# Query turns moved into the projection banks, between the gate tiles

## The reference

```
h = rmsnorm(x, norm1_g)
q, k, v, cb, cc, cx, g_attn, g_conv = split(h @ w_in)
q, k = partial_rope(rmsnorm(q)), partial_rope(rmsnorm(k))
attn = windowed_gqa(q, k, v, sink)      # 8 heads, 2 KV heads, band of 3 blocks of 128
conv = cb * conv3(cc * cx)
merged = sigmoid(g_attn) * (attn @ w_attn_proj) + sigmoid(g_conv) * (conv @ w_conv_proj)
x = x + merged @ w_out
x = x + hierarchical_moe(rmsnorm(x))
```

## Time and profile before

| quantity | value |
|---|---|
| median of 3 runs | 2042.31 us (2041.8 to 2044.8) |
| profiled execution, its own time | 2044.8 us |
| its span | 2043.0 us |
| TensorE busy with matmuls | 1889.1 us, 92% |
| VectorE, ScalarE, GpSimd busy | 49%, 40%, 28% |
| granted TensorE clock, mean | 0.973 of full speed |

### The profile page before, as it was taken

How to read it: one execution, slowest core, us unless ns; L and a number is a source line. 1 busy time by engine, 2 the same in 40 slices (tenths; PEclk the granted TensorE clock), 3 DMA queues, 4 the chain that set the end, 5 groups by cost and what they waited for, 6 DMA issues and landing times.

```text
span 2043.0 us, 27997 instructions
## 1 busy us (share of the span) xinstructions
PE 1889.1 (92%) x10942; PEld 1470.2 (72%) x10942; DVE 1004.2 (49%) x1998; ACT 815.1 (40%) x1506; POOL 567.7 (28%) x403
## 2 busy tenths in 40 slices
PE   7999999998785999988999999999789999999997
PEld 6878879832221793457888888888767797888886
DVE  2160443521111525963366677822466714776777
ACT  5123551211111423264455444342266725454442
POOL 2244332011111220144422113243045543113211
PEclk9999999998988999999999999999899999999999
DMA  6223103699998330201123223321500012223321
GB/s 231 83 84 123 42 1 145 274 388 419 420 420 317 104 106 18 83 1 43 42 83 124 83 83 124 130 60 42 124 2 1 2 42 78 88 83 124 124 83 42
DMA packets 82324, 248.48 MB, mean 122 GB/s; under 512 B 12259, under 2 KB 15523, under 8 KB 69904
## 3 DMA queue, kind: packets, MB, share of 16 engines
q1 hardware_dynamic: 75936, 231.54, 30.6%
q0 software_dynamic: 4880, 9.89, 1.4%
q10 hardware_dynamic: 1376, 5.25, 0.6%
HBM read 241.89 MB, written 12.58 MB: 125 GB/s over the span
## 4 chain that ended last, share of the span: by engine, by line
PE 48%; DVE 4%; issue 2%; ACT 2%; POOL 0%; DVEq 0%; ACTq 0%
PE psA L1427 33%; PE psT L1585 2%; PE psS L1585 2%; PE psO L1585 2%; PE psO L1967 2%; PE psT L2004 1%; DVE x L2556 1%; PE psS L1995 1%; PE psA L1536 1%; PE psO L1487 1%; PE psT L1519 1%; PE psA L1995 1%; DVE scr L3390 1%; ACT big L2037 1%; PE psA L1911 1%
## 5 line engine op out<-in xcount | busy, mean ns | idle before, releaser
L1136 POOL TENSOR_TENSOR w_slot<-ring,w_slot 128x1024 fp32r<-128x1024 f32 (+2 forms) x80 | 208.5, 2619 | 542.3 <-ACT w_slot L2037 542.0
L1427 PE MATMUL psA<-hT_hi,w_slot 128*128 128x512 f32 x992 | 307.9, 389 | 0.0
L2037 ACT ACTIVATE w_slot<-ring 128x1024 fp32r<-128x1024 f32 (+2 forms) x178 | 192.0, 1088 | 176.9 <-PE psA L1427 77.0
L1427 PEld LDWEIGHTS psA<-hT_hi,w_slot 128*128 128x128 f32 x992 | 186.3, 188 | 38.7
L1427 PE MATMUL psA<-hT_lo,w_slot 128*128 128x512 f32 x496 | 192.9, 389 | 0.0
L2556 DVE TENSOR_TENSOR x<-psA,x 128x512 f32<-128x512 f32 (+1 forms) x204 | 121.0, 622 | 146.3 <-PE psA L1427 142.5
L2556 DVE TENSOR_TENSOR w_slot<-ring,w_slot 128x1024 fp32r<-128x1024 f32 x98 | 119.8, 1224 | 116.1 <-ACT w_slot L2037 116.1
L2037 ACT ACTIVATE big<-psA 128x512 f32<-128x512 f32 (+6 forms) x149 | 66.2, 469 | 272.0 <-PE psA L1427 140.2
L1427 PE MATMUL psA<-w_slot,hid_part 128*128 128x512 f32 x672 | 161.4, 389 | 0.0
L2037 ACT ACTIVATE scr<-scr,stat 128x384 f32<-128x384 f32 (+3 forms) x224 | 124.4, 556 | 71.2 <-DVE stat L3390 39.4
L1427 PEld LDWEIGHTS psA<-w_slot,hid_part 128*128 128x128 f32 x672 | 126.2, 188 | 26.1
(11 more groups left out here) (378 smaller groups left out, 4427.5 us busy)
## 6 DMA issues: line engine op xcount, KB each, us to landing
ring<-in_mlp_w SPq DMA_DIRECT2D x32, 2048.0 KB, 8.2
ring<-in_w_in SPq DMA_DIRECT2D x8, 2048.0 KB, 8.0
ring<-in_w_gate_e SPq DMA_DIRECT2D x14, 1024.0 KB, 17.1
ring<-in_w_up_e SPq DMA_DIRECT2D x14, 1024.0 KB, 21.6
ring<-in_w_down_e SPq DMA_DIRECT2D x13, 1024.0 KB, 27.2
big<-in_w_down_e SPq DMA_DIRECT2D x12, 1024.0 KB, 27.5
ring<-in_ab_w_in SPq DMA_DIRECT2D x5, 2048.0 KB, 8.0
scr<-in_w_down_e SPq DMA_DIRECT2D x7, 1024.0 KB, 24.9
```

What stands on the lines that cost most here:

```text
L1136: nc.gpsimd.tensor_tensor(part(w_lo, c), raw_piece(c), part(w_hi, c).bitcast(F32), ALU.subtract)\
L1427: ins = pe.matmul(o, a, b, start=(at == 1), stop=(at == 3 * len(terms)))
L2037: return nc.scalar.activation(o, i, f, **kw)
```

## The change

The six turns become jobs in psA0 and psA1, and stand between the gate tiles: q turns 0 and 1, gate tile 0, q turns 2 and 3, gate tile 1, both k turns, gate tile 2. ScalarE reads them out in the same order. VectorE's last operation on each turn now raises `proj_evacuated`, in place of `query_lo`; TensorE waits before the attention until both k turns are read out. In all, ten jobs stand where four stood, so later jobs keep their banks.

The last gate tile gets the sigmoid function at step 2 of the attention, as the other tiles; VectorE's addition and reciprocal go away. The small operation that loads the exponential's table early goes away. The four casts `conv_hi` on VectorE move from steps 3 to 6, one each, to steps 2 and 3, two each.

```diff
-               ("gc0", 4), ("gc1", 4), ("mergec", KD), ...
+               ("gc0", 4), ("turn_qa", 2), ("gc1a", 1), ("turn_qb", 2), ("gc1b", 1), ("turn_qc", 2), ("gc1c", 2), ("mergec", KD), ...
+def second_gate(m):
+    return JOBS["gc1" + "abcc"[m]] + m // 3
+def query_turn(j):
+    return JOBS["turn_q" + "abc"[j // 2]] + j % 2
...
 # TensorE
             pe.wait_ge(heads_ready, 1)
             for j in range(4):
-                for t in range(NT):
-                    ins = pe.transpose(query_bank(j)[:, t * P:(t + 1) * P], qk[:, t, j * P:(j + 1) * P], ident)
-                ins.then_inc(query_turned, 1)
+                turn(query_turn(j), [qk[:, t, j * P:(j + 1) * P] for t in range(NT)])
+                if j % 2:
+                    gate_tile(j // 2)
             for g in range(2):
-                for t in range(NT):
-                    for half in range(2):
-                        ins = pe.matmul(query_bank(4 + g)[HD * half:HD * (half + 1), t * P:(t + 1) * P],
-                                        qk[:, t, 512 + HD * g:512 + HD * (g + 1)], ident, start=True, stop=True)
-                ins.then_inc(query_turned, 1)
-            for m in range(3):
-                gate_tile(m)
-            pe.wait_ge(query_lo, 6)
+                turn_twice(query_turn(4 + g), [qk[:, t, 512 + HD * g:512 + HD * (g + 1)] for t in range(NT)])
+            gate_tile(2)
+            copied_all(pe, "turn_qc", 2)
...
 # ScalarE
             for j in range(4):
-                act.wait_ge(query_turned, j + 1)
-                A(band_q[0:HD, j, :], query_bank(j)[0:HD, :], ACT.Copy)
-                A(band_q[HD:P, 4 + j, :], query_bank(j)[HD:P, :], ACT.Copy).then_inc(stack_hi, 1)
-            act.wait_ge(query_turned, 6)
+                n = query_turn(j)
+                product(act, n)
+                A(band_q[0:HD, j, :], bank(n)[0:HD, :], ACT.Copy)
+                A(band_q[HD:P, 4 + j, :], bank(n)[HD:P, :], ACT.Copy).then_inc(stack_hi, 1)
+                if j % 2:
+                    conv_gate(1, j // 2)
+            product(act, query_turn(5))
             for g in range(2):
-                A(band_k[:, g, 0, :], query_bank(4 + g)[:, :], ACT.Copy).then_inc(stack_hi, 1)
-            for m in range(3):
-                conv_gate(1, m)
-            A(small[:, 310:311], ident[:, 0:1], ACT.Exp)
+                A(band_k[:, g, 0, :], bank(query_turn(4 + g))[:, :], ACT.Copy).then_inc(stack_hi, 1)
+            conv_gate(1, 2)
...
                 if step == 2:
-                    evac(JOBS["gc1"] + 3, gc[:, KD - 1, :], f=ACT.Exp, scale=-1.0)
+                    conv_gate(1, 3)
...
 # VectorE, for each turn: the last lo operation
-                    .then_inc(query_lo, 1)
+                    .then_inc(proj_evacuated[n % 2], 1)
...
-                if 3 <= step < 7:
-                    if step == 3:
-                        product(dve, JOBS["gc1"] + 3)
-                    copied(dve, JOBS["cb"] + step - 3)
-                    nc.vector.tensor_copy(conv_hi[:, step - 3, :], conv[:, step - 3, :]).then_inc(conv_in_hi, 1)
-                if step == 9:
-                    copied(dve, JOBS["gc1"] + 3)
-                    link(ts(gc[:, KD - 1, :], gc[:, KD - 1, :], 1.0, op0=ALU.add))
-                    link(nc.vector.reciprocal(gc[:, KD - 1, :], gc[:, KD - 1, :]))
+                if step in (2, 3):
+                    if step == 2:
+                        product(dve, second_gate(3))
+                    for m in range(2 * step - 4, 2 * step - 2):
+                        copied(dve, JOBS["cb"] + m)
+                        nc.vector.tensor_copy(conv_hi[:, m, :], conv[:, m, :]).then_inc(conv_in_hi, 1)
```

More of the change, by code:

```diff
@@ L138 @@
                ("norm0", KD), ("kv", NT), ("q", 2 * NT), ("cc", 4), ("cx", 4), ("cb", 4), ("ga", KD),
-               ("gc0", 4), ("gc1", 4), ("mergec", KD), ("turn_o0", 4), ("mergea", KD), ("wo", 3 * NT), ("tail1", NT + KD),
+               ("gc0", 4), ("turn_qa", 2), ("gc1a", 1), ("turn_qb", 2), ("gc1b", 1), ("turn_qc", 2), ("gc1c", 2), ("mergec", KD), ("turn_o0", 4), ("mergea", KD), ("wo", 3 * NT), ("tail1", NT + KD),
                ("ranks", 1), ("table", 1), ("moe", 5 * PAIRS),
@@ L154 @@
 SPLIT_NORMS = (3, 4, 5)
+def second_gate(m):
+    return JOBS["gc1" + "abcc"[m]] + m // 3
+def query_turn(j):
+    return JOBS["turn_q" + "abc"[j // 2]] + j % 2
 def job(stage, i):
+    if stage == "gc1":
+        return second_gate(i)
     if stage == "nq":
@@ L485, in build @@
         stack_hi = sem("stack_hi")
-        query_turned = sem("query_turned")
-        query_lo = sem("query_lo")
         p_scores = sem("p_scores")
@@ L661, in ax_bank @@
             return (psT + psO)[t]
-        def query_bank(j):
-            return (psT + psO + psS)[j]
         def index_bank(c):
@@ L1607, in gate_tile @@
                 wh, wl = piece(SPLIT_AT["gc1"] + m)
-                split_product(JOBS["gc1"] + m, T, [(wh[:, k, :], wl[:, k, :], hT_hi[:, k, :], hT_lo_early[:, k, :])
+                split_product(second_gate(m), T, [(wh[:, k, :], wl[:, k, :], hT_hi[:, k, :], hT_lo_early[:, k, :])
                                                   for k in range(KD)])
@@ L1630, in conv_gates @@
                 if step == CONV_STEP:
-                    copied_all(pe, "gc1", 4)
+                    copied_all(pe, "gc1c", 2)
                     pe.wait_ge(conv_in_hi, 4)
@@ L2232, in conv_gate @@
             def conv_gate(c, m):
-                evac(JOBS[f"gc{c}"] + m, gc[:, 4 * c + m, :], f=ACT.Sigmoid)
+                evac(job(f"gc{c}", m), gc[:, 4 * c + m, :], f=ACT.Sigmoid)
                 then_split(SPLIT_AT[f"gc{c}"] + m)
@@ L2891, in _ @@
             for j in range(4):
+                n = query_turn(j)
                 dve.wait_ge(stack_hi, j + 1)
-                tt(band_q[HD:P, j, :], query_bank(j)[0:HD, :], band_q[0:HD, j, :].bitcast(F32), ALU.subtract)
-                tt(band_q[0:HD, 4 + j, :], query_bank(j)[HD:P, :], band_q[HD:P, 4 + j, :].bitcast(F32), ALU.subtract)\
-                    .then_inc(query_lo, 1)
+                tt(band_q[HD:P, j, :], bank(n)[0:HD, :], band_q[0:HD, j, :].bitcast(F32), ALU.subtract)
+                tt(band_q[0:HD, 4 + j, :], bank(n)[HD:P, :], band_q[HD:P, 4 + j, :].bitcast(F32), ALU.subtract)\
+                    .then_inc(proj_evacuated[n % 2], 1)
             for g in range(2):
+                n = query_turn(4 + g)
                 dve.wait_ge(stack_hi, 5 + g)
-                tt(band_k[:, g, 1, :], query_bank(4 + g)[:, :], band_k[:, g, 0, :].bitcast(F32), ALU.subtract).then_inc(query_lo, 1)
+                tt(band_k[:, g, 1, :], bank(n)[:, :], band_k[:, g, 0, :].bitcast(F32), ALU.subtract)\
+                    .then_inc(proj_evacuated[n % 2], 1)
             def conv_part(step):
-                if 3 <= step < 7:
-                    if step == 3:
-                        product(dve, JOBS["gc1"] + 3)
-                    copied(dve, JOBS["cb"] + step - 3)
-                    nc.vector.tensor_copy(conv_hi[:, step - 3, :], conv[:, step - 3, :]).then_inc(conv_in_hi, 1)
-                if step == 9:
-                    copied(dve, JOBS["gc1"] + 3)
-                    link(ts(gc[:, KD - 1, :], gc[:, KD - 1, :], 1.0, op0=ALU.add))
-                    link(nc.vector.reciprocal(gc[:, KD - 1, :], gc[:, KD - 1, :]))
+                if step in (2, 3):
[4 more added lines that the diff above has]
+                        nc.vector.tensor_copy(conv_hi[:, m, :], conv[:, m, :]).then_inc(conv_in_hi, 1)
                 m = (step - CONV_STEP) // 3 - 1
```

## The result

| | before | after |
|---|---|---|
| device time, median of 4 runs each (us) | 2042.05 (2039.28 to 2044.8) | 2057.86 (2056.71 to 2058.74) |
| ratio, 95% interval | | 1.0083 [1.0067, 1.0098] |
| profiled execution (us) | 2044.8 | 2061.94 |
| its span, its mean granted TensorE clock | 2043.0, 0.973 | 2060.1, 0.968 |

The changed kernel is slower, by 17.0 us by the ratio (13.7 to 20.0). The forecast was +11.4 (2053.7 us) with a range up to 2056.8. The direction and the three waits came as forecast; the size did not, and the median lies 1.06 us outside the range. Each profiled execution is the slowest of its kernel in this comparison; they lie 17.1 us apart.

A forecast was written before the change was run, and what follows sets the result against it. TensorE was taken to set the pace, with no gap. Stalls 8.4, clock 2.3, table load 1.3 and reciprocal -0.6 sum to +11.4 us, on the median 2042.3 giving 2053.7 us; range for 8 in 10 is 2050.3 to 2056.8.

The forecast's parts named there:

- The three stalls: Before gate tiles 0, 1 and 2, TensorE waits for shared banks to be read; +8.4 us in sum, 7.4 to 9.4 allowed.
- The third table load: In the attention's head, the load after the sigmoid stands on ScalarE's path and shifts the attention; +1.3 us.
- The reciprocal's 0.6 us: In the attention, removing VectorE's reciprocal on the last gate tile gives back 0.59 us; -0.6 us in the sum.
- signs of being wrong: Gate tile 1 starting before 208 us, or the shift at the first score not found again at the end.
- The clock: TensorE's clock falls behind both query-turn stalls, 1.15 us each, +2.3 us; nothing for the k turns.
- The clock does not fall behind the stalls: Rival for the query-turn stalls: no clock fall, or only in their idle part; +9.1 us, 2051.4 us; chance 0.22.
- The stalls are worse: Rival: both clock falls in full, casts and a slower table switch on the path; +14.5 us, 2056.8 us; chance 0.12.
- a slower switch of tables: In the attention's head, a drain of about 1.38 us on every switch would make the table-load term 2.7 us.
- the casts: At step 2, VectorE's two casts put item 3's mask about 0.9 us later; hidden, otherwise up to 0.9 us.
- Absorbed: Rival: a load behind the attention that comes at its own time absorbs the delay; 2042 to 2045 us; chance 0.03.
- faster: Rival: all of ScalarE's 3.02 us wait for the reciprocal comes back and stalls do not exist; 2040.6 us; chance 0.02.
- both falls behind the stalls to be sure: At the query-turn stalls, if transposes do not count as clock work, both falls are sure; sum up by at most 0.8 us.

The follow-up runs named there:

- experiment 4: The changed kernel with twelve unused matmuls of 512 columns before gate tiles 0 and 1 each; 2055.64 us, +12.1 us against the kernel before.
- experiment 12: The changed kernel with unused filler matmuls in the query-turn waits, attention head, behind the attention and around the MLPs; 2049.95 us, +6.9 us against the kernel before.
- experiment 2: The kernel before with only the last gate changed: sigmoid, two casts per step, no add, reciprocal or early table load; 2046.22 us, +3.1 us.
- experiment 7: The kernel before without the addition and reciprocal of the last gate tile, so part of the gate is wrong; 2044.40 us, +1.2 us (-0.6 to 2.9).
- experiment 1: The changed kernel with the old last gate, casts and early table load, so only the turns moved; 2057.17 us, +13.5 us against the kernel before.
- experiment 5: The kernel before with the sigmoid gate and its table loads, no reciprocal, casts one per step; 2047.54 us, +3.9 us.
- experiment 9: The kernel before with one 128x1 Sigmoid ahead of ScalarE's evacuation at step 2, two more table loads in its wait; 2043.71 us, +0.8 us (-1.0 to 2.7).
- experiment 10: The kernel before with one 128x1 Sigmoid right behind ScalarE's evacuation at step 2, two more table loads on its path; 2046.42 us, +4.3 us.
- experiment 3: The kernel before with gate tiles between the turns as in the changed kernel, but turns in their own banks; 2041.91 us, -0.6 us (-2.4 to 1.2).
- experiment 8: The kernel before with unused 160-column matmuls around the turns behind the attention and before both MLPs' first products; 2037.06 us, -5.5 us.
- experiment 11: The kernel with only the turns moved, ScalarE reading each turned tile before the weight piece; 2052.85 us, +10.0 us against the kernel before.

## Why the prediction was wrong

**Right.** The three stalls, place by place: 2.89, 2.88 and 1.51 us of waiting where about 2.9, 2.8 and 1.4 were forecast, and together they put the first score back by 8.8 us, without the clock, instead of 8.4. That sum was built from the rows of this place in their new order, with the hand-over lag of 0.05 us from another layer where such turns share a bank, and experiments 4 and 12 confirm it. The third table load was priced at 1.3 us and took 1.4: item 5, still ahead of the low stretch, comes 10.84 us behind the first score instead of 9.45. The reciprocal's 0.6 us stand in the traces of experiments 2 and 7 to the tenth, though no median can show them. One of the prediction's own signs of being wrong did come: the shift at the first score, 10.9 us, is not the one at the end, 17.1. Most of the difference arises in the head and behind the attention; at 300 us the shift is 16.5. Nothing behind absorbed the delay: the queue's wait for the merge product, 92.5 us in the earlier trace rows, is no shorter now, 98.1:

```profile
SPq L1125 <- PE psA L1433: 98.1, 1, 98.1
```

**The step that failed** is the term "The clock", priced at 2.3 us; the trace pair has about 7.3 us for it: 2.5 at the turns, 3.1 in the attention's head and 1.7 behind the attention. It looked for falls only behind the two stalls of the query turns. There it was nearly right in size: 2.5 us in the changed kernel (one fall of 6.8 us, and none behind the first stall), about 3 in experiment 1 (two falls). That size is partly luck in the changed kernel: one fall of twice the length came in place of two. What it left out are the falls at places where the change adds no stall of microseconds:

- The head of the attention. The prediction counted the third table load by its 1.28 us alone. TensorE's work there is short matmuls with waits of 0.5 to 0.9 us between; the load makes them a little sparser, and the clock falls for 6.8 us. The trace of the changed kernel has 3.1 us for it, beside 1.4 for the load (4.5 at item 10). Experiments 2 and 5 show the same without the moved turns, and 9 and 10 show that a longer path on ScalarE does it.
- The turns behind the attention. The earlier trace rows were read as the price of a fall, but not as a place where the fall can get longer: 3.4 us low before, 10.2 us now, 1.7 us more by the 49th matmul. Experiment 1 has 6.8 us there and 1.1 us more. Why it gets longer is open: the change adds no wait there, and traces of kernels with neither the moved turns nor the sigmoid differ there too (3.4 us before, 6.8 in experiments 3 and 9, none in 7).

**How much of the 17 us is clock.** Twice the missing share of the granted clock times the span is the time spent at 1.2 GHz: 108 us for the kernel before (mean over 29 runs), 119 for the turns alone, 126 for the changed kernel (mean of seven executions at 0.968 to 0.972), 87 for experiment 8 and 92 for experiment 12. At most half of such a time is lost, where TensorE sets the pace. The changed kernel has 18 us more of it, worth up to 9 us. Waits, load and reciprocal are 8.8 + 1.4 - 0.6 = 9.6, and 17.0 - 9.6 leaves 7.4. That is within the bound, and near the 7.3 of the traces, but the clock's share was shown by removal only in part: the fillers of experiment 4 brought 2.5 us in the trace and took 17.0 to 12.1 in the ratios; all of them (experiment 12) took 17.0 to 6.9, which is 4.6 us more than the 5.5 that such fillers bring in the kernel before.

**The rivals.** "The clock does not fall behind the stalls" is out, by experiment 1. "The stalls are worse", at 2056.8, came nearest in size and mostly for a wrong reason: its 3.1 us for two full falls are what experiment 1 shows, but the rest of its extra came from a slower switch of tables and from the casts. In the changed kernel the load at 234.84 takes 1.28 us and the next activation starts at 236.13, so there is no drain of 1.38 us such as the Trainium skill gives in "ScalarE: Activation LUTs", section "What ACT_TABLE_LOAD costs"; and experiment 5 clears the casts. "Absorbed" and "faster" are out. From the rule of the Trainium skill that transposes do not count as work for the clock ("TensorE: Matmul & The Clock Gate", section "Part 4: PE-mode transpose") the prediction took both falls behind the stalls to be sure. Both came in experiment 1, but the profiled execution of the changed kernel kept 1.00 behind the first stall, so that conclusion does not hold; the rule itself was not tested:

```profile
200.00:205.00 5.00, 4.72 (x20) 3.87 (x21) 1.51 (x3) 0.00 (x0) 0.12 (x1) 1.00 0.63 255
```

**Still open.** Which of the falls come in a given execution: a profile shows one. In experiments 2 and 10 the traces are 5.7 and 6.6 us later than before at the 49th matmul behind the last turns, counted from the first score, and the ratios show 3.1 and 4.3. Behind 320 us, where the kernels without fillers run the same instructions, most traces have 106.7 to 106.9 us at the low clock, but 99.9, 96.5 and 103.3 in experiments 2, 9 and 10. Half of such a difference is 2 to 5 us of time, and the 2 us of experiment 12 are of this size.

## What to carry to other kernels

A bank that is read by two engines in turn must not be the one that the next product needs: the readers' lag, 10 us of slack before, became 8.8 us of waiting, with not one instruction added. When a change makes TensorE's work sparser anywhere, price the clock at every place where the trace has it idle in short pieces or already low, not only behind the new waits; here it came to some 7 us beside 8.8 us of waits. And look for such places in the kernel that you have: fillers of 160 columns, in gaps TensorE had anyway, made it 5.5 us faster.

## What the hardware showed that was not expected

The clock fell behind eight transposes and a wait of 1.94 us (experiment 11, the second time and not the first), and in the attention's head behind waits of 0.94, 0.78 and 0.52 us with short matmuls between them, where the kernel before, with two waits of 0.52 us, kept 1.00. Executions of one kernel differ in it: 0.971 to 0.976 for the kernel before, and its times go with it from 2046 to 2038 us.

VectorE's casts to fp32r become slow beside GpSimd's subtractions. In the changed kernel the second pair takes 2.51 us where the first takes 0.76; four subtractions of GpSimd run from 235.10 us on:

```profile
234.59 0.76 DVE L2912 CAST conv_hi<-big 128x512 fp32r<-128x512 f32 x2
235.67 2.51 DVE L2912 CAST conv_hi<-big 128x512 fp32r<-128x512 f32 x2
...
235.10 5.45 POOL L1155 TENSOR_TENSOR conv_lo<-big,conv_hi 128x512 fp32r<-128x512 f32 x4 [12.34 <-DVE conv_hi L2912]
```

Before, one cast to a step took 0.42 to 0.60 us each, and 0.42 each in experiment 5, where every cast starts when no subtraction runs. That the two share something was not tested by itself.
